# Two recurrences and attention on one core: an attention tile as one piece in every third step, recurrence outputs in one step

## The reference, cut to what matters

```
s = (jnp.einsum('bqhd,bkhd->bhqk', qn_b, k_nope)
     + jnp.einsum('bqhd,bkd->bhqk', qr_b, k_rope))
p = jax.nn.softmax(s.astype(jnp.float32) * scale, axis=-1)
return jnp.einsum('bhqk,bkhd->bqhd', p.astype(v.dtype), v)
```

```
sa = jnp.einsum('bhvk,bhk->bhv', state, a_t)
state = (state * w_t[:, :, None, :] + sa[..., None] * b_t[:, :, None, :]
         + v_t[..., None] * k_t[:, :, None, :])
return state, jnp.einsum('bhvk,bhk->bhv', state, r_t)
```

## Time and profile before

| | |
|---|---|
| median of 3 runs | 3516.8 us (3514.44 to 3517.77) |
| the profiled execution's own time | 3505.72 us |
| its span | 3503.9 us |
| mean granted TensorE clock | 0.991 |
| PE, weight loads, DVE, ACT, POOL busy | 96%, 76%, 49%, 32%, 9% |
| this stage | from about 541 to 1338 us |

### The profile page before, as it was taken

How to read it: one execution, slowest core, us unless ns; L and a number is a source line. 1 busy time by engine, 2 the same in 40 slices (tenths; PEclk the granted TensorE clock), 3 DMA queues, 4 the chain that set the end, 5 groups by cost and what they waited for, 6 DMA issues and landing times.

```text
span 3503.9 us, 61009 instructions
## 1 busy us (share of the span) xinstructions
PE 3366.8 (96%) x27176; PEld 2664.1 (76%) x27176; DVE 1713.8 (49%) x2537; ACT 1112.9 (32%) x1799; POOL 322.6 (9%) x342
## 2 busy tenths in 40 slices
PE   8989998999999999999999999999999999999998
PEld 7678776777766785587888888787778788888877
DVE  5353564665666666654345434642554522352236
ACT  4323424444444331132124212432333311241124
POOL 1131241111111222000000000001000000000000
PEclk9999999999999999999999999999999999999999
DMA  3241253111210304421112211332003111121113
GB/s 143 67 149 43 72 189 107 59 38 41 71 59 31 113 21 151 144 84 49 49 48 96 73 48 48 108 104 98 25 31 120 63 51 49 61 96 55 49 67 107
DMA packets 89973, 269.84 MB, mean 77 GB/s; under 512 B 11552, under 2 KB 12080, under 8 KB 89712
## 3 DMA queue, kind: packets, MB, share of 16 engines
q1 hardware_dynamic: 78960, 230.29, 19.9%
q0 software_dynamic: 10752, 35.66, 3.0%
HBM read 219.77 MB, written 46.14 MB: 76 GB/s over the span
## 4 chain that ended last, share of the span: by engine, by line
PE 82%; DVE 10%; ACT 4%; issue 2%; DMA 1%; POOL 0%; SPq 0%; DVEq 0%; ACTq 0%; POOLq 0%
PE ps L355 77%; PE ps L354 3%; DVE SM L375 2%; PE ps L358 2%; DVE AR L364 2%; ACT HT L1148 1%; DVE X L364 1%; DVE HT L368 1%; DVE W L364 1%; ACT AR L361 1%; ACT WS L361 0%; DVE WS L364 0%; DVE EX L364 0%; ACT W L2074 0%; DMA qk_d<-AR 0%
## 5 line engine op out<-in xcount | busy, mean ns | idle before, releaser
L355 PE MATMUL ps<-HH,WS 128*128 128x512 f32 (+1 forms) x3232 | 997.6, 390 | 0.0
L355 PEld LDWEIGHTS ps<-HH,WS 128*128 128x128 f32 (+1 forms) x3232 | 605.2, 187 | 128.9
L355 PE MATMUL ps<-HL,WS 128*128 128x512 f32 x1616 | 637.7, 395 | 6.3 <-DVE HL L364 5.9
L364 DVE TENSOR_TENSOR WS<-W,WS 128x1024 fp32r<-128x1024 f32 x244 | 300.2, 1230 | 617.8 <-ACT WS L361 617.8
L361 ACT ACTIVATE WS<-W 128x1024 fp32r<-128x1024 f32 x244 | 256.6, 1051 | 843.4 <-PE ps L355 836.7
L355 PE MATMUL ps<-WS,SA 128*128 128x512 f32 x2112 | 486.7, 392 | 13.6 <-DVE SA L364 11.0
L355 PEld LDWEIGHTS ps<-WS,SA 128*128 128x128 f32 x2112 | 397.4, 189 | 101.1 <-issue 15.2
L355 PEld LDWEIGHTS ps<-HL,WS 128*128 128x128 f32 x1616 | 302.6, 187 | 71.6 <-issue 6.8
L355 PE MATMUL ps<-AR 64*64 64x64 f32 (+2 forms) x5440 | 200.1, 240 | 17.2 <-ACT AR L361 9.6
L364 DVE TENSOR_TENSOR SA<-HA,SA 128x512 fp32r<-128x512 f32 x176 | 121.5, 692 | 187.3 <-ACT SA L361 187.3
L355 PE MATMUL ps<-HL,HI 128*128 128x512 f32 (+1 forms) x512 | 208.1, 406 | 3.6 <-POOL WL L364 2.8
(11 more groups left out here) (286 smaller groups left out, 4354.1 us busy)
## 6 DMA issues: line engine op xcount, KB each, us to landing
W<-in_w_fd SPq DMA_DIRECT2D x88, 512.0 KB, 3.4
AR<-rw_d SPq DMA_DIRECT2D x104, 256.0 KB, 4.1
W<-in_w_fg SPq DMA_DIRECT2D x44, 512.0 KB, 3.4
W<-in_w_fu SPq DMA_DIRECT2D x44, 512.0 KB, 3.4
W<-in_w_tok SPq DMA_DIRECT2D x24, 512.0 KB, 3.5
rw_d<-X POOLq DMA_DIRECT2D x40, 256.0 KB, 3.4
X<-in_x SPq DMA_DIRECT2D x16, 512.0 KB, 8.9
W<-in_w_g SPq DMA_DIRECT2D x16, 512.0 KB, 3.7
```

The source lines that it names most:

```text
L355: return pe.e.matmul(o, l, r, start=start, stop=stop)
L364: return e.e.tensor_tensor(o, x, y, op)
```

## The change

`att_steps` yields once for each tile instead of after each of scores, transposes and value product: piece i holds scores of tile i, transposes of tile i-1 and, for odd i from 3, a value product. On ACT (`copies_first`) the copies of tile i-1 stand ahead of the exponential of tile i in the piece. Attention is taken in every third round (`one_of_three`), and in every other one of the first seven steps. In the recurrence, O's two banks, its products with the state and those with `v` move from the step of U to the last step, ahead of its products with U.

```diff
-        def att_steps(scores, transp, pv, load):
+        def att_steps(scores, transp, pv, load, copies_first=False):
             load(0)
             yield
             for i in range(66):
                 if i % 8 == 4 and i // 8 + 1 < 8:
                     load(i // 8 + 1)
-                if i < 64:
+                if i < 64 and not copies_first:
                     scores(i)
-                    yield
                 if 1 <= i <= 64:
                     transp(i - 1)
-                    yield
+                if i < 64 and copies_first:
+                    scores(i)
                 if i % 2 and i >= 3:
                     pv((i - 3) // 2)
-                    yield
+                yield
...
-            return att_steps(scores, transp, pv, skip)
+            return att_steps(scores, transp, pv, skip, copies_first=True)
...
-                    bo = take(pe, PEs, "O", i, u, n=2)
-                    state(pe, c, bo, u, 1)
                     b = take(pe, PEs, "U", i, u)
                     pe.wait_ge(*at(AEs, "Y", i, u))
                     pe.wait_ge(*at(VEs, "B", i, u))
...
                     x.then_inc(*pe.sig(PEs, "U", i, u))
-                    b = bo
+                    yield
+                    b = take(pe, PEs, "O", i, u, n=2)
+                    state(pe, c, b, u, 1)
                     for h in range(4):
                         cc = (4 * u + h) * 64
                         rows_by(pe, b, h, c.M4[:, h, 3, :], v_[:, cc:cc + 64], False)
-                    yield
                     pe.wait_ge(*at(AEs, "U", i, u))
...
-            for _ in range(7):
+            for n in range(7):
                 next(s0)
-                next(at_)
-            interleave(s0, s1, at_)
+                if n % 2 == 0:
+                    next(at_)
+            interleave(s0, s1, one_of_three(at_))
             e.close("scans", e.name)
+
+        def one_of_three(gen):
+            for _ in gen:
+                yield
+                yield
+                yield
```

## The result

| | before | with the change |
|---|---|---|
| median | 3516.5 us (20 runs, 3507.8 to 3520.9) | 3523.0 us (20 runs, 3516.7 to 3531.5) |
| profiled execution, time and span | 3505.7, 3503.9 us | 3520.4, 3518.6 us |
| its mean granted clock | 0.991 | 0.989 |

The ratio is 1.0023, interval 1.0016 to 1.003: slower by 0.2%, 6.5 us between the medians. The forecast was 3532 us. Its direction and its main term came out; its size didn't: 15.9 us were forecast on top of the kernel before, and 6.5 lie between the medians.

The account below looks back on a forecast made before the run. TensorE, busy 96% of the span, was taken as the bound. Piece terms of 35.7 us replace 28.8, with +8 for outputs and +1 for lead-in: +15.9 us, about 3532 us, range 3493 to 3556.

Parts of the forecast that it names:

- Transposes behind scores: In the attention piece, TensorE's transposes wait for VectorE's scaling of the previous tile on 42 of 63 tiles: +28.7 us.
- ScalarE in the piece: On even tiles, copies ahead of the exponential delay ScalarE's later copies for the recurrences: +11.5 us (0 to 25).
- Banks: PSUM banks still read when retaken: +5 us, 7 of 32 even pieces; as rival, most even pieces, 3554 us, chance 0.12.
- Credit: In the round after each attention piece, the plain waits are hidden, 0.15 us in each of 63: -9.5 us.
- Outputs: In the recurrences' U step, O's moved products no longer cover ScalarE's copy, 0.85 us a time: +8 us (0 to 14).
- the ring: The cyclic order in which `take` hands out eight PSUM banks; the forecast followed it for attention's even pieces.
- Lead-in: Three attention pieces leave the first seven steps, where one recurrence runs alone: +1 us (-2 to +4).
- likeliest case: The forecast itself for the whole kernel: slower by +7 to +30 us, 3524 to 3547 us, chance 0.38.
- VectorE gets ahead: Rival: in the two rounds without attention VectorE clears its list, transposes wait only 14 us; 3497 us, chance 0.27.
- The terms cancel: Rival: transposes wait 18 us and outputs cost 3, so the sum is near 0; 3517 us, chance 0.23.

Follow-up runs that it names:

- the scaling two rounds later: Changed kernel with VectorE's reciprocal and scaling of a tile moved out of the piece to two rounds behind it, a round ahead of its transposes: 3492.9 us, ratio 0.9938.
- run with banks held: Kernel before with O's products moved to the last step, but O's two banks still taken in the step with U: 3516.8 us, ratio 0.9999.
- the scaling one round later: Changed kernel with VectorE's scaling of a tile moved out of the piece to one round behind it: 3516.2 us, ratio 1.0002.

## Why the prediction was right in direction and how its terms came out

**Transposes behind scores, +28.7: right**, to 28.5 us, and shown by removal: without it the kernel is 30 us faster. This term alone makes the change a loss; the rest of it is worth 23 us.

**ScalarE in the piece, +11.5: not there.** The forecast said that the copies push the exponential to 4.2 us behind the scores' start and with it ScalarE's later copies for the recurrences. The mean over 63 tiles is 4.03 us (3.74 before). But it is the late scaling that pushes: with the scaling two rounds later and ScalarE's order unchanged the mean is 3.69, since the copies run while ScalarE would stand in front of the exponential for the maximum anyway. And where the price was to appear, in PE's waits for ACT AR, 15.2 us became 14.5. The mechanism exists (ScalarE late on tiles without a value product), but it is the other order that sets it off.

**Banks, +5: about right**: 3.0 us of waits for ACT HT are left. The Trainium skill, page Perfetto Trace Analysis, section Optimization Strategy, says that repeated gaps can mean that there isn't enough PSUM for the next tile. The run with banks held agrees with that for the kernel before (5 us between two kernels whose intervals just overlap), but the repeated gap after the change is VectorE's.

**Credit, -9.5: right in kind, read too high.** In the round right behind a piece PE waits for nothing but the 3.0 us of the banks, so its plain waits are hidden, as the forecast said. But the period of the earlier trace rows holds 2.9 us of standing (63.21 us less 60.32 busy), not 4.3, so a round hides 0.10 us and 63 of them 6.5.

**Outputs, +8: the term that failed.** Its mechanism is there, behind the short U step, at 0.61 us a time in place of 0.85. But the forecast counted it alone and set the gain of the edit at nothing; it had left out the ring. Where there is attention the edit gives 7.5 us in the run of this part alone, 6 of them by the banks, and by the medians it gives 4 us in all. With the change, 33 rounds fewer lie behind the last value product. Up to PE's wait of 1.76 us they take 76.2 us, and 33 rounds of 2.257 us more would make 150.7, against 149.8 before: 0.9 us of the term.

**Lead-in, +1: right.** The first round of `interleave` comes 0.8 us earlier, and one tile's scores (1.9 us) more lie behind it.

**The sum.** The two profiled executions lie 14.7 us apart (3505.7 and 3520.4), which looks like the forecast of 15.9, but that is luck in which executions were profiled: the one of the kernel before lay 11.1 us under its median, with a granted clock of 0.991, the one with the change 2.6 us under its own, with 0.989. In 29 runs of the kernel before the fastest five (3504.5 to 3508.2 us) have 0.989 to 0.991 and the slowest five (3520.8 to 3523.0) 0.986 or 0.987, some 3 us for each 0.001; at 0.988 the medians are 3516.1 before and 3523.1 with the change. So it was right to put 11.1 us on top to reach the median, and what is too high in 3532 is the sum of the terms: 15.9 for 6.5. The measured 3523.0 us lie just under the likeliest case's own range of 3524 to 3547.

The traces say where. The stage grew by 11.2 us. Of these 7.5 were there by PE's wait of 1.76 us near its end (at 1330.34 before and 1337.00 with the change, 6.7 apart, which agrees with the medians); the other 3.7 came in the last 12 us, of which the trace with the change has 9.7 at half clock and the one before none, behind waits that are the same but for 0.1 us. Counted as the forecast counted it (187 rounds of 2.257 us, 61 scores, 62 transposes and 32 value products in the 697.4 us up to the last value product), attention costs 33.5 us beyond its own work: 28.8 before, 35.7 forecast, and 5.7 with the scaling two rounds later. So the terms of the piece came near as a sum (33.5 for 35.7, with the outputs' gain in it, and with waits in the rounds that no term names in place of ScalarE's 11.5), and most of the excess is the outputs' 8 us.

**Rivals.** "VectorE gets ahead" needed a wait under 0.20 us a tile; it was 0.45. It is the right picture of the kernel with the scaling moved (3492.9 against 3497). "Banks" is refuted: it needed over 25 us of PE's waits for ACT HT, and there are 3.0. "The terms cancel" (3517) is nearer in time than the forecast (6 us off in place of 9), but its condition, 18 us in front of the transposes, isn't met (28.5).

**What a wait costs beyond its number.** The stage less PE's standing and half of the half-clock time is 713 us before and 712 with the change, but 703 to 706 in the kernels in which the scaling was moved and the piece kept, so some 8 of the 30 us are not in the list of waits. They are in the pieces. Timeline of PE with the change, a piece without a wait and one with a wait:

```profile
612.97 1.98 PE L355 MATMUL ps<-HT 96*128 96x512 f32 x4
614.79 1.04 PE L358 MATMUL ps<-CS,HT 128*128 128x128 f32 x8
...
633.62 1.98 PE L355 MATMUL ps<-HT 96*128 96x512 f32 x4
636.08 1.07 PE L358 MATMUL ps<-CS,HT 128*128 128x128 f32 x8 [0.48 <-DVE HT L368]
```

Without a wait the transposes start 1.82 us behind the scores, before the record of the scores ends; with it 2.46. So a printed wait of 0.48 us costs 0.64, and 41 times 0.16 make 6.6 us, an estimate from these two pieces.

What stays open: which places of standing bring the clock down (see below), and what the pieces would do without the outputs' part.

## What to carry to other kernels

When work is merged into one piece, ask for each engine what stands in its list between an operation and whoever needs it: an operation is free where a piece of the bound engine's work lies between the two, and moving it one round (0.75 us of VectorE work) decided 23 us here. Put into an engine's wait whatever doesn't depend on it, as the copies ahead of the exponential (9 us, and 29 with the scaling moved). And before a profiled execution is set against a median, compare their granted clocks.

## What the runs showed of the hardware

**Standing can cost a second time, in the clock.** With the change, PE was busy 0.98 us of 3.4, then the next 3.4 us ran at half clock:

```profile
567.60:571.00 3.40, 0.98 (x8) 0.86 (x8) 3.36 (x4) 0.56 (x2) 3.07 (x2) 1.00 0.00 0
571.00:574.40 3.40, 3.40 (x33) 3.28 (x32) 0.15 (x2) 1.86 (x4) 0.00 (x0) 0.50 0.00 0
```

The standing there is the longest of the 41 waits for the scaling, 2.8 us. The other 40 are of 0.3 to 1.9 us, and from 574 to 1339 us the clock didn't fall. With the scaling one round later PE stood 7 us less in all, but 16 times for over 1 us (29.9 us together; with the change 13 times, 21.1 us), and 40 us more of the stage ran at half clock. That the gathering decides is not shown, though: the kernel before stood 22 times for over 1 us (27.8 us) and had 6.8 us at half clock.

**VectorE's scaling takes 0.75 us beside an idle GpSimd** (0.752 to 0.756 in 46 of 64) and up to 1.56 beside GpSimd's products, as in the rows at 782.60 above; over the stage 7.9 of the 28.5 us are this stretch. The Trainium skill, page SBUF — State Buffer, section SBUF: two separate sides, says that the two engines share a pair of ports and that, for some kinds of VectorE operation, the one that comes second is fully blocked until the other's instruction ends. The trace agrees in kind in that row: GpSimd starts 0.03 us ahead of the scaling and ends at 783.61, and the scaling ends 0.55 us behind it. Had it been blocked fully, it would have needed its whole 0.75 from there.
